# Half of a PEER expert layer's tokens: 256 gathered rows per table replaced by both 16,384-row tables read whole and multiplied densely

## What is computed

```python
vals, idx = lax.top_k(s, PEER_TOPK)                    # 16 of 128, twice
sc, pos = lax.top_k(cand.reshape(..., 256), PEER_TOPK) # 16 of the pairs
ex = jnp.take_along_axis(cand_idx..., pos, axis=-1)    # 0 .. 16383
g = jax.nn.softmax(sc, axis=-1)
act = jax.nn.gelu(jnp.einsum('chkd,cd->chk', u[ex], hc), approximate=False)
return jnp.einsum('chk,chkd->cd', g * act, v[ex])
```

## Time and profile before

| | |
|---|---|
| median of 3 runs (lowest to highest) | 2162.14 us (2156.3 to 2166.65) |
| span of the profiled execution | 2163.3 us |
| PE, PEld | 1761.0 us (81%), 878.7 us (41%) |
| DVE | 1313.0 us (61%) |
| ACT | 622.7 us (29%) |
| POOL | 1165.7 us (54%) |
| moved by DMA | 659.72 MB, mean 305 GB/s |
| mean granted clock of PE | 0.920 |

### The profile page before, as it was taken

The page is one execution under the profiler, slowest core; times in us unless marked ns, Lnnn a source line. Parts: engine busy times, 40 slices in busy tenths (PEclk is TensorE's granted clock), DMA queues, the critical chain, the costliest instruction groups (busy, mean ns, idle before and its releaser), DMA issues.

```text
span 2163.3 us, 25921 instructions
## 1 busy us (share of the span) xinstructions
PE 1761.0 (81%) x8598; PEld 878.7 (41%) x8598; DVE 1313.0 (61%) x3436; ACT 622.7 (29%) x1489; POOL 1165.7 (54%) x1555
## 2 busy tenths in 40 slices
PE   7998899988888979798888777767777676777776
PEld 2544445777756434344443223223223222232322
DVE  1289853777656857555565575656756556755553
ACT  3256413454543322222222212221222212221121
POOL 2100004556535556666666666666666666666664
PEclk9999999999999989999998888879988888988899
DMA  7456454545398899999999999999999999999997
GB/s 244 134 199 225 147 185 122 147 113 142 84 323 307 309 342 377 355 382 395 385 389 358 371 360 374 359 363 391 355 368 372 362 373 363 379 359 367 366 366 290
DMA packets 282158, 659.72 MB, mean 305 GB/s; under 512 B 71248, under 2 KB 120496, under 8 KB 282032
## 3 DMA queue, kind: packets, MB, share of 16 engines
q0 software_dynamic: 150336, 552.67, 67.3%
q1 hardware_dynamic: 131696, 105.46, 16.3%
HBM read 635.49 MB, written 22.54 MB: 304 GB/s over the span
## 4 chain that ended last, share of the span: by engine, by line
PE 35%; issue 13%; POOL 8%; DMA 6%; another core or an unknown queue 5%; DVE 3%; ACT 2%; SPq 0%; ACTq 0%; POOLq 0%; DVEq 0%
PE banks L2046 27%; POOL arena L1623 8%; DMA arena<-in_peer_v_dram,arena 4%; PE banks L2067 3%; PE banks L559 2%; DVE arena L1986 1%; PE banks L1525 1%; DMA arena<-in_peer_u_dram,arena 1%; PE banks L2117 1%; DMA arena<-in_w_out_dram 1%; ACT arena L1682 0%; PE banks L2075 0%; ACT L1779 0%; ACT L1704 0%
## 5 line engine op out<-in xcount | busy, mean ns | idle before, releaser
L2046 PE MATMUL banks<-arena 128*128 128x512 f32 x1984 | 1000.7, 656 | 309.2 <-issue 235.7
L2046 PEld LDWEIGHTS banks<-arena 128*128 128x128 f32 x1984 | 397.0, 208 | 899.9 <-issue 829.0
L1986 DVE CUSTOM_DVE_ANT_0 arena<-arena,banks 128x1024 f32<-128x1024 f32 x512 | 615.9, 1217 | 232.3 <-DMA arena<-in_peer_u_dram,arena 193.3
L1623 POOL DMA_INDIRECT arena<-in_peer_v_dram,arena x504 | 474.5, 942 | 356.3 <-issue 132.4
L1623 POOL DMA_INDIRECT arena<-in_peer_u_dram,arena x512 | 482.1, 942 | 175.8 <-issue 151.8
L1682 ACT ACTIVATE arena<-arena 128x128 f32<-128x128 f32 x496 | 183.0, 398 | 881.0 <-remote 318.4
L1137 PE MATMUL banks<-arena 64*64 64x64 f32 (+1 forms) x2688 | 109.0, 232 | 13.9 <-POOL arena L791 6.2
L2657 PE MATMUL banks<-arena 128*128 128x512 f32 x224 | 111.7, 606 | 0.7 <-ACT arena L2315 0.7
L1137 PEld LDWEIGHTS banks<-arena 64*64 64x64 f32 x2688 | 96.5, 137 | 28.7 <-issue 12.5
L2753 PE MATMUL banks<-arena 128*128 128x512 f32 x192 | 86.9, 609 | 1.2 <-issue 1.2
L2067 PE MATMUL banks<-arena 128*128 128x384 f32 x256 | 85.5, 485 | 0.8 <-issue 0.8
(11 more groups left out here) (342 smaller groups left out, 2068.6 us busy)
## 6 DMA issues: line engine op xcount, KB each, us to landing
arena<-in_w_mod_dram SPq DMA_DIRECT2D x18, 1024.0 KB, 7.4
arena<-in_peer_wq_dram SPq DMA_DIRECT2D x16, 1024.0 KB, 11.1
arena<-in_w_in_dram SPq DMA_DIRECT2D x27, 512.0 KB, 7.8
arena<-in_peer_u_dram,arena POOLq DMA_INDIRECT x512
arena<-in_peer_v_dram,arena POOLq DMA_INDIRECT x512
arena<-in_w_mod_dram SPq DMA_DIRECT2D x3, 2048.0 KB, 11.4
bk_scratch<-arena POOLq DMA_DIRECT2D x8, 768.0 KB, 3.9
kr_scratch<-arena POOLq DMA_DIRECT2D x8, 768.0 KB, 6.0
```

The costliest lines, as they stand in the source:

```text
L1623: pool.indirect_dma_start(ring[:, j % RING, :], None, table, bass.IndirectOffsetOnAxis(ap=idx[:, hi % 4, j:j + 1].bitcast(U32), axis=0)).t ...
L1986: nc.vector.tensor_tensor_reduce(u_ring[:, j % RING, :], u_ring[:, j % RING, :], h2cur, 1.0, 0.0, ALU.mult, ALU.add, acts[:, h % 2, j:j + ...
L2046: m = nc.tensor.matmul(PO[h][:, :], diag[:, j % 4], v_ring[:, j % RING, 512 * h:512 * h + 512], start=hp == 0 and j == 0, stop=hp == HEADS ...
```

## The change

Tiles 0 and 1 (16 heads) keep the scheme of rows and gathers, with rings of 6 and 5 places, and tiles 2 and 3 (256 tokens) get another one. Both tables are read whole by SP in 128 blocks of 128 consecutive rows (512 KB each) through three places, `u` first and then `v`:

- For a block of `u`, PE transposes it in 8 pieces (`turn_block`), ACT moves these to SBUF in four steps (`move_turns`), PE multiplies them with the 256 tokens in 8 products of 256 columns (`score_block`), ACT takes the gelu of the 128x256 result (`block_gelu`), and SP writes that to memory (`act_save`). It is a dense matrix of experts by tokens.
- DVE chooses experts for the 16 heads of tiles 2 and 3 as before, during heads 4 to 7 (`dense_topk`). It splits their numbers into key and row, and for 8 tokens at a time makes one-hot rows by comparison (`mark_picks`: 128x256, 128x1024, and one multiplication of 128x256). PE multiplies these in 8 products with 128x128 weights and 32 columns (`make_weights`), which gives the weight of each expert for each token, and ACT moves it (`move_weights`). There are 128 such groups, 32 for each of four parts.
- For a block of `v`, SP loads the saved gelu (`act_load`), DVE multiplies it by the weights (`weigh_block`), and PE adds the block in 4 products of 512 columns into banks 0 to 3 (`add_block`).

All of it is interleaved by a count of units. A unit is one slot of one of the 16 remaining heads, 256 in all. Units 48 to 165 take the 128 blocks of `u`, units 133 to 230 the weights, and units 167 to 254 the 128 blocks of `v`. The last head has no split between PE and DVE any more.

Core of the diff (new functions, and PE's loop over the units; removed lines are left out):

```diff
 SUB = 16
 TRI = DH // SUB * (SUB * DH + SUB)
-RING = 8
+URING, VRING = 6, 5
+DENSE = 2 * P
+BLOCKS = KEYS
...
+PART = 32
+PARTS = KEYS // PART
+GROUP = 8
+GROUPS = DENSE // GROUP
+HELD = 8
+ROUNDER = 1.5 * 2.0 ** 30
 
...
+    def turned_by(u):
+
+        return max(0, min(BLOCKS + 1, ((BLOCKS + 1) * (u + 1 - TURN_AT)) // (DENSE_AT - TURN_AT)))
+
+    def built_by(u):
+
+        if u < DENSE_AT:
+            return max(0, (GROUPS * (u + 1 - BUILD_AT)) // (DENSE_AT - BUILD_AT))
+        part, i = divmod(u - DENSE_AT, 22)
+        return min(GROUPS * PARTS, GROUPS * (part + 1) + min(GROUPS, (GROUPS * (i + 1)) // AGAIN))
+
+    def weighted_by(u):
+
+        return max(0, min(BLOCKS, (16 * (u + 1 - DENSE_AT)) // 11))
+
+    def added_by(u):
+
+        return weighted_by(u - 1)
+
+    def steps(by, u):
+
+        return range(by(u - 1), by(u))
+
+    def products_at(j):
+
+        return min(NSL, (NSL * max(j - 1, 0) + 14) // 15)
+
...
+        def block_load(y):
+
+            if y >= BLOCKS + 3:
+                sp.wait_ge(dense_added, y - BLOCKS - 2)
+            elif y >= 3:
+                sp.wait_ge(blocks_turned, 4 * (y - 2))
+            src = u_blocks[y] if y < BLOCKS else v_blocks[y - BLOCKS]
+            sp.dma_start(blocks[:, y % 3], src).then_inc(block_loaded[y % 3], 16)
+
+        def act_save(b):
+
+            sp.wait_ge(acts_made, b + 1)
+            sp.dma_start(act_dram[b], saving[:, b % 2]).then_inc(acts_saved[b % 2], 16)
+
+        def act_load(b):
+
+            if b >= HELD:
+                sp.wait_ge(dense_added, b - HELD + 1)
+            sp.wait_ge(acts_saved[b % 2], 16 * (b // 2) + 16 + SAVES_BEFORE)
+            sp.dma_start(held[:, b % HELD], act_dram[b]).then_inc(acts_held[b % HELD], 16)
+
...
+        def move_turns(x):
+
+            for k in range(4):
+                act.wait_ge(blocks_turned, 4 * x + k + 1)
+                if x >= 2 and k == 0:
+                    act.wait_ge(blocks_scored, x - 1)
+                nc.scalar.activation(turned[:, x % 2, 2 * k:2 * k + 2], v3(psum[4 + k % 2][:, 0:2 * P]),
+                                     ACT.Identity).then_inc(turns_moved, 1)
+
+        def block_gelu(b):
+
+            act.wait_ge(blocks_scored, b + 1)
+            if b >= 2:
+                act.wait_ge(acts_saved[b % 2], 16 * (b // 2) + SAVES_BEFORE)
+            nc.scalar.activation(saving[:, b % 2], psum[3][:, 0:DENSE], ACT.Gelu).then_inc(acts_made, 1)
+
+        def move_weights(q):
+
+            part, i = divmod(q, GROUPS)
+            if q == GROUPS:
+                act.wait_ge(output_stored, 16)
+            act.wait_ge(pick_products, q + 2)
+            nc.scalar.activation(weights[part % 2][:, :, GROUP * i:GROUP * i + GROUP].rearrange("p c n -> p n c"),
+                                 weight_bank(q)[:, 0:GROUP * PART].rearrange("p (n c) -> p n c", c=PART),
+                                 ACT.Identity).then_inc(pick_moves, 1)
...
+        def mark_picks(q):
+
+            part, i = divmod(q, GROUPS)
+            tokens = slice(GROUP * i, GROUP * i + GROUP)
+            keys, rows = picked_keys[:, q % 2], picked_rows[:, q % 2]
+            if q == 0:
+                dve.wait_ge(pick_moves, 2)
+            if q >= 2:
+                dve.wait_ge(pick_products, q)
+            nc.vector.tensor_tensor(rows, row_iota[:, PART * part:PART * part + PART].unsqueeze(1).broadcast_to([P, GROUP, PART]),
+                                    picks[:, 0, tokens].unsqueeze(2).broadcast_to([P, GROUP, PART]), ALU.is_equal).then_inc(pick_steps, 1)
+            nc.vector.tensor_tensor(keys, key_iota.unsqueeze(1).broadcast_to([P, GROUP, KEYS]),
+                                    picks[:, 1, tokens].unsqueeze(2).broadcast_to([P, GROUP, KEYS]), ALU.is_equal).then_inc(pick_steps, 1)
+            dve.wait_ge(pick_steps, PICK_STEPS + 3 * q + 1)
+            nc.vector.tensor_tensor(rows, rows, picks[:, 2, tokens].unsqueeze(2).broadcast_to([P, GROUP, PART]),
+                                    ALU.mult).then_inc(pick_steps, 1)
+
+        def weigh_block(b):
+
+            part, c = divmod(b, PART)
+            dve.wait_ge(acts_held[b % HELD], 16 * (b // HELD) + 16 + HELD_BEFORE[b % HELD])
+            if c == 0:
+                dve.wait_ge(pick_moves, GROUPS * (part + 1) + 2)
+            nc.vector.tensor_tensor(held[:, b % HELD], held[:, b % HELD], weights[part % 2][:, c], ALU.mult).then_inc(acts_weighted, 1)
...
+        def turn_block(x, k):
+
+            if k == 0:
+                pe.wait_ge(block_loaded[x % 3], 16 * (x // 3) + 16 + BLOCKS_BEFORE)
+                if x == 0:
+                    pe.wait_ge(dots, 3 * NSL)
+                    pe.wait_ge(h2_current, 2)
+            if 4 * x + k >= 2:
+                pe.wait_ge(turns_moved, 4 * x + k - 1)
+            for i in range(2):
+                at = P * (2 * k + i)
+                m = nc.tensor.transpose(psum[4 + k % 2][:, P * i:P * i + P], blocks[:, x % 3, at:at + P], ident)
+            m.then_inc(blocks_turned, 1)
+
+        def score_block(b, k):
+
+            if k == 0 and b:
+                pe.wait_ge(acts_made, b)
+            pe.wait_ge(turns_moved, 4 * b + k + 1)
+            for i in (2 * k, 2 * k + 1):
+                m = nc.tensor.matmul(psum[3][:, 0:DENSE], turned[:, b % 2, i], h2T[:, i, P:3 * P], start=i == 0, stop=i == KT - 1)
+            if k == 3:
+                m.then_inc(blocks_scored, 1)
+
+        def turn_picks():
+            pe.wait_ge(pick_steps, PICK_STEPS)
+            for i, src in enumerate((place_rows, flat_places, flat_scores)):
+                for t in range(2):
+                    m = nc.tensor.transpose(psum[i // 2][:, DENSE * (i % 2) + P * t:DENSE * (i % 2) + P * t + P], src[:, P * t:P * t + P], ident)
+            m.then_inc(pick_products, 1)
+
+        def make_weights(q):
+
+            pe.wait_ge(pick_steps, PICK_STEPS + 3 * q + 3)
+            if q >= 2:
+                pe.wait_ge(pick_moves, q + 1)
+            for i in range(GROUP):
+                m = nc.tensor.matmul(weight_bank(q)[:, PART * i:PART * i + PART], picked_keys[:, q % 2, i], picked_rows[:, q % 2, i],
+                                     start=True, stop=True)
+            m.then_inc(pick_products, 1)
+
+        def add_block(b):
+
+            pe.wait_ge(block_loaded[(BLOCKS + b) % 3], 16 * ((BLOCKS + b) // 3) + 16 + BLOCKS_BEFORE)
+            pe.wait_ge(acts_weighted, b + 1)
+            if b == 0:
+                pe.wait_ge(pick_moves, 2)
+            for t in range(2):
                 for h in range(2):
+                    m = nc.tensor.matmul(psum[2 * t + h][:, :], held[:, b % HELD, P * t:P * t + P],
+                                         blocks[:, (BLOCKS + b) % 3, 512 * h:512 * h + 512], start=b == 0, stop=b == BLOCKS - 1)
+            m.then_inc(dense_added, 1)
+
+        pe.wait_ge(mixer_moved, 1)
+        experts(0, range(8))
+        pe.wait_ge(mixer_moved, 2)
+        project_out(3, 0)
+        experts(0, range(8, NSL))
+
+        columns(1)
+        columns(2)
+        experts(1, range(NSL))
+        columns(3)
+
...
+        for u in range(TURN_AT, UNITS):
+            g, j = divmod(u, NSL)
+            now = range(products_at(j), products_at(j + 1))
+            if g == 9 and j == 1:
+                pe.wait_ge(final_vector, 2)
+            experts(g - 1, now)
+            scored, asked = late_now(g, j)
+            if scored is not None:
+                late_scores(scored)
+            if asked is not None:
+                late_query(asked)
+            for x in steps(turned_by, u):
+                for k in range(4):
+                    if x < BLOCKS:
+                        turn_block(x, k)
+                    if x:
+                        score_block(x - 1, k)
+            if u == PREPARE_AT + 2:
+                turn_picks()
+            for q in steps(built_by, u):
+                make_weights(q)
+            for b in steps(added_by, u):
+                add_block(b)
+        experts(SLOTS - 1, range(NSL))
```

843 lines of the change are left out of this document (449 added, 394 removed).

## The result

The changed kernel takes 2763.62 us (median of 4 runs, 2751.32 to 2776.63), and the kernel before took 2164.39 us beside it (2156.3 to 2169.07). The ratio is 1.2785, with a 95% interval of [1.2725, 1.2845]: 599 us slower. The profiled execution has a span of 2775.0 us and took 2776.63 us, so it stands 13 us above the median, at the top of the runs.

What follows compares the result with a forecast made beforehand. PE was to replace DMA as the bound: 808 us start + 1707 PE work + 135 waits + 10 joint and head changes + 11 end = 2671, said as 2670 us (1.235 times before). Own range 2570 to 2760, whole range 2510 to 2790.

Steps and rivals of the forecast that it cites:

- What bounds it: From 802 us on, PE gets 787 us more work against 441 us of room and replaces DMA as the bound.
- PEclk under 0.9: Sign that would show the forecast wrong: PE's granted clock below 0.9, where near 1.00 was expected.
- Start of the work at 808 us: Unit 48, the fourth head's start: 802 us before, plus 6 us for smaller rings, later first gathers and block loads.
- PE's prices: PE's work from unit 48 on, priced per record or product at full clock: 1707 us, or 1608 with cheap weights.
- the upper end for the weights: The 1024 32-column products: 0.22 us each taken, 225 us, between bounds of 126 and 235 us.
- Waits: PE waiting on ACT: 105 us at 110 units' diagonals, 7 for gelu only, 23 for table loads; 135 us in all.
- All these are at full clock: Statement that the record and product times used to price PE's work hold at PE's full clock.
- small holes in the second stretch: Allowance of 40 us in the upper side of the forecast's range, for the stretch with the blocks of `v`.
- slower transposes: Allowance of 50 us in the upper side of the range, for transposes of 0.17 us in pairs.
- The rival on the clock: Holes of about 1 us lower PE's clock to 0.86 in the first stretch: 150 us more, 2820 us; chance 0.13.
- PE without waits: PE is the bound but its queue runs ahead of ACT: 2437 us at the bottom, some 2500 mid; chance 0.14.
- DMA as the bound: DMA stays the bound and the kernel gets 272 us faster, to 1890 us; chance 0.02.

Runs made afterwards that it cites:

- e2: Changed kernel with the 1024 products for the weights 128 columns wide, not 32 (weights not the layer's): 2673.01 us, ratio 1.3105 to the kernel before.
- e5: Changed kernel with the products for the weights 64 columns wide, not 32 (weights not the layer's): 2681.56 us, ratio 1.2406 to the kernel before.
- e6: Changed kernel with ACT's next diagonals ahead of the block's gelu and 128-column products for the weights: 2558.69 us, ratio 1.1832 to the kernel before.
- a1: The changed kernel unaltered, measured a third time, on a chip where the kernel before takes 2037.54 us: 2754.74 us, ratio 1.3498.
- e3: Changed kernel with ACT building the next unit's diagonals ahead of the block's gelu, nothing left out: 2589.2 and 2586.55 us, ratios 1.2714 and 1.2692.
- e7: Changed kernel with dense products cut as in e4 and ACT's diagonals ahead of the gelu: 1993.91 us, ratio 0.9218 to a before of 2162.23.
- e4: Changed kernel with dense products cut to about a quarter, all transfers kept (outputs wrong): 2081.26 us, ratio 1.0212 to a before of 2038.01.

## Why the prediction was right, and where its size was off

- **What bounds it.** Right. PE is busy 0.88 to 0.90 of the time up to 1900 us (over 90% was named) and without a gap from 2100 us on, and the bytes are not what is waited for: DMA share 0.51 to 0.64 up to 2500 us against "about 0.6". But "PEclk under 0.9", one of the prediction's own signs of being wrong, did appear: 0.88 from 1570 to 1900 us.
- **Start of the work at 808 us.** The first transpose starts at 809.7.
- **PE's prices.** Transposes 0.11 a record (0.12 taken), 256 columns 0.215 (0.43 a product), 512 columns 0.435 a record (0.43), the weights 0.109 a record (0.11 taken, of bounds 0.061 and 0.115). The choice of the upper end for the weights was right. The rule of the Trainium skill (TensorE: Matmul & The Clock Gate, LDWEIGHTS), by which the estimate was 219 us, agrees with the 2048 x 0.109 = 223 us measured, and with the fact that 128 columns cost no more (0.111).
- **Waits.** Right, but 106.8 us of idle time is not the same thing as the 105 us of the sum. It leaves out the 0.17 us for which the last record stays open (110 x 0.17 = 19 us), and it holds the table loads of the exponentials, for which the sum had 23 us apart: in e2 95 of the 110 places have 0.8 to 0.9 us and 15 have 1.5 to 2.7 us. Like for like, 107 + 19 = 126 us stand against 105 + 23 = 128, and e5 to e6 measured 123. `add_block` waits for nothing, as worked out from DVE and DMA.
- **The sum held for a full clock.** e2 has all the records and waits of the changed kernel, a clock of 0.99 to 1.00 in these stages, and a span of 2674.1 us against the sum's 2671.
- **The step that was off** is the sentence "All these are at full clock", with the own range's "small holes in the second stretch (40)". The clock was the missing term, worth 82 us (a1 to e2) or 85 us (the changed kernel to e5, on one chip). By stretches, from the first start of line 2340 in a1 and e2 (1908.2 and 1881.6): a1 is 27 us behind there (33 us counted from the first transpose, 797.3 and 803.8), and 2755.5 - 2674.1 - 26.6 = 55 us are lost after it. In e2 the second stretch begins 20 us later than the sum has it (808 + 918 + 135 = 1861) and is 17 us shorter (2674.1 - 1881.6 - 11 = 782 against 799), so that the sum comes out so near is partly luck: these two errors cancel, and what the 20 us are was not followed. The 2764 us lie just above the forecast's own range (to 2760), and inside the whole one. That too is partly luck: of the way up to 2790, 90 us had been added for slower transposes (50) and small holes in the second stretch (40), and neither came. Most of the 93 us are clock.
- **The rival on the clock** had the right direction and the wrong cause and place. It put a clock of 0.86 on the first stretch, on account of the holes, for 150 us. From 850 to 1570 us the holes were there and the clock was 0.98 to 1.00, much as the window with 70% busy time had said. The prediction read that window as "short holes", but it has a single hole of 2.96 us, and the window with 0.51 one of 4.93 us, so neither was like this stretch. The fall came with the 32-column products, which the prediction priced for their time alone. The Trainium skill's statement (TensorE: Matmul & The Clock Gate, PE-mode transpose) that transposes don't count as the clock sees PE busy made nothing here that could be seen: with 8 transposes in each block that stretch held its clock.
- **PE without waits** (2437 to 2500 us) and **DMA as the bound** (1890 us) did not occur. e3 shows what the first would take: another order on ACT.
- **Where the gain of the change went.** By the prediction's sum it takes 272 us of transfers away and gives PE 787 us. With a quarter of the products and another order e7 is 168 us faster than the kernel before on its chip. e4, without that order and on one of the faster chips, is 43 us slower.

**What stays open.** Why the clock falls with 32-column products, and why in units 133 to 165 only together with the holes, was not taken further than these runs: they show at which widths it falls, not by what the chip decides. Why the kernel before differs by 6% between chips, and what e7 gains where it takes 2038 us, is open too. The 9 us between 2754.74 and 2763.62 us are within what the runs scatter (2738.81 to 2776.63).

## What to carry to other kernels

Before a gather is replaced by a dense product, hold the time that its records add to PE against PE's free time, and not only the bytes saved against the bandwidth: here 787 us (worked out in the prediction) went into 441 us of room. When PE is the bound, look for whatever stands ahead of PE's next operand in another engine's list and itself waits for PE's last result; to move the diagonal of the next row ahead of the gelu gave 168 us of 2755, some 45 of them clock. And where many products load full weights and stream few columns, try them wider even if the columns are thrown away: the record took as long, and the kernel was 41 us faster (85 us in the old order, in e5, which computes other weights).
